# Mixer projections with tokens on partitions and 512 weight columns moving, raw residual in, scaling and turning behind, and a per-boundary table of begin beats

## What is computed

```python
for l in range(2):                                 # first stack
    h = h + 0.5 * swiglu(rmsnorm(h, ffn1_norm[l]), ...)
    z = rmsnorm(h, mix_norm[l]) @ w_in[l]          # 1024 x 5536
    # latent attention (8 heads), differential attention (8 heads), pooling
    branches = einsum('bsnc,ncd->bsnd', [y_mla, y_diff, y_pool], w_branch[l])
    h = h + sum_n(sigmoid(z_gate[n]) * branches[n]) @ w_out[l]
    h = h + 0.5 * swiglu(rmsnorm(h, ffn2_norm[l]), ...)
h = rmsnorm(h, final_norm)
for l in range(2):                                 # second stack
    x = x + 0.5 * rms_norm(swiglu_2(rms_norm(x, pre), ...), post)
    proj = rms_norm(x, ln_mix_pre[l]) @ w_in_2[l]  # windowed attention, mLSTM, RWKV-7
    x = x + rms_norm(concat(y_attn, y_mlstm, y_rwkv) @ w_out_2[l], post)
    x = x + 0.5 * rms_norm(swiglu_2(...), post)
    gate = sigmoid(rms_norm(x, ln_ple_pre[l]) @ w_ple_gate[l])
    x = x + rms_norm(gate * (p[l] @ w_ple_proj[l]), post)
```

## Time and profile before

| | |
|---|---|
| Three runs | 2524.03, 2524.66, 2525.28 us (median 2524.66) |
| The profiled execution | 2525.72 us, its span 2524.4 us |
| PE busy | 2396.8 us, 95% of the span, 13760 matmuls |
| DVE, ACT busy | 1516.1 us (60%), 1224.8 us (49%) |
| Granted TensorE clock, mean | 0.968 |
| Stages, from the ends of the residual's last writes | `mix1` 243.9 and 245.4 us, `mix2` 206.8 and 205.9 us, FFNs 185 to 208 us, `ple` 45.1 and 36.7 us |

### The profile page before, as it was taken

How to read it: one execution, slowest core, us unless ns; L and a number is a source line. 1 busy time by engine, 2 the same in 40 slices (tenths; PEclk the granted TensorE clock), 3 DMA queues, 4 the chain that set the end, 5 groups by cost and what they waited for, 6 DMA issues and landing times.

```text
span 2524.4 us, 33723 instructions
## 1 busy us (share of the span) xinstructions
PE 2396.8 (95%) x13760; PEld 2026.4 (80%) x13760; DVE 1516.1 (60%) x2356; ACT 1224.8 (49%) x2095; POOL 53.7 (2%) x66
## 2 busy tenths in 40 slices
PE   8999999999999999999999979999979997999997
PEld 6788899888888889988788868778857886877885
DVE  4556786555655677755555574755555557476555
ACT  4445454544544555544544443554454444355444
POOL 0000000000000000000000000000000000000000
PEclk9999999999999999999999989799999998979999
DMA  6554345555555433555455532255544552214553
GB/s 238 189 187 155 106 137 189 175 183 197 176 187 182 138 117 132 181 188 197 169 183 185 175 93 91 63 173 181 194 146 160 194 181 87 90 63 171 184 191 113
DMA packets 110746, 400.11 MB, mean 158 GB/s; under 512 B 12288, under 2 KB 12672, under 8 KB 110336
## 3 DMA queue, kind: packets, MB, share of 16 engines
q1 hardware_dynamic: 110592, 397.96, 47.0%
HBM read 396.86 MB, written 1.05 MB: 158 GB/s over the span
## 4 chain that ended last, share of the span: by engine, by line
PE 84%; DVE 10%; ACT 4%; issue 1%; DMA 1%; POOL 0%; SPq 0%; ACTq 0%; DVEq 0%
PE ps L369 75%; DVE wlo L361 3%; PE ps L651 2%; ACT whi L354 1%; PE ps L1814 1%; DVE alo L511 1%; PE ps L1263 1%; ACT ahi L488 1%; PE ps L472 1%; PE ps L1228 1%; PE ps L1247 0%; PE ps L1219 0%; PE ps L2184 0%; DVE xs L767 0%; PE ps L2302 0%
## 5 line engine op out<-in xcount | busy, mean ns | idle before, releaser
L361 DVE TENSOR_TENSOR wlo<-raw,whi 128x1024 fp32r<-128x1024 f32 (+1 forms) x748 | 886.9, 1211 | 172.0 <-ACT whi L354 166.1
L354 ACT CAST whi<-raw 128x1024 fp32r<-128x1024 f32 (+1 forms) x748 | 758.1, 1042 | 125.1 <-PE ps L369 124.7
L369 PE MATMUL ps<-whi,ahi 128*128 128x512 f32 (+2 forms) x1632 | 655.4, 402 | 50.4 <-DVE alo L511 42.5
L369 PE MATMUL ps<-whi,alo 128*128 128x512 f32 (+2 forms) x1632 | 638.4, 391 | 0.0
L369 PE MATMUL ps<-wlo,ahi 128*128 128x512 f32 (+2 forms) x1632 | 637.3, 390 | 0.0
L369 PEld LDWEIGHTS ps<-whi,ahi 128*128 128x128 f32 x1632 | 311.4, 191 | 122.2 <-issue 43.2
L369 PEld LDWEIGHTS ps<-whi,alo 128*128 128x128 f32 x1632 | 310.7, 190 | 63.3
L369 PEld LDWEIGHTS ps<-wlo,ahi 128*128 128x128 f32 x1632 | 312.0, 191 | 56.7
L369 PE MATMUL ps<-whi,yhi 128*128 128x512 f32 (+1 forms) x852 | 335.9, 394 | 0.9 <-DVE wlo L361 0.9
L369 PE MATMUL ps<-whi,ylo 128*128 128x512 f32 (+1 forms) x852 | 332.3, 390 | 0.0
L369 PE MATMUL ps<-wlo,yhi 128*128 128x512 f32 (+1 forms) x852 | 332.2, 390 | 0.0
(11 more groups left out here) (363 smaller groups left out, 2340.2 us busy)
## 6 DMA issues: line engine op xcount, KB each, us to landing
raw<-stream SPq DMA_DIRECT2D x718, 512.0 KB, 4.2
raw<-stream SPq DMA_DIRECT2D x16, 388.0 KB, 2.9
bcb<-bcs SPq DMA_DIRECT2D x9, 512.0 KB, 4.5
raw<-stream SPq DMA_DIRECT2D x8, 416.0 KB, 3.8
raw<-stream SPq DMA_DIRECT2D x4, 384.0 KB, 3.2
cst<-consts SPq DMA_DIRECT2D x1, 1260.0 KB, 8.4
msc<-misc SPq DMA_DIRECT2D x1, 1160.0 KB, 7.5
xs<-xin SPq DMA_DIRECT2D x2, 512.0 KB, 4.3
```

What stands on the lines that cost most here:

```text
L354: act.do.copy(whi[:, n % NSP, 0:w], raw[:, n % NRAW, 0:w]).then_inc(*rounded(n))
L361: dve.do.tensor_tensor(wlo[:, n % NSP, 0:w], raw[:, n % NRAW, 0:w], whi[:, n % NSP, 0:w].bitcast(F), ALU.subtract).then_inc(*rest(n))
L369: m = pe.do.matmul(o, a, b, start=(first and q == 0), stop=(last and q == n - 1))
```

## The change

- `scaled` and `xn` are gone: both mixers turn the raw `xs`, as the FFNs do. The row scale is applied where a projection leaves PSUM (`scale(i)`), in the tanh (`hst`, half the scale) or in the sigmoid.
- All projections of the mixers and `w_branch` have tokens stationary and up to 512 weight columns moving. `pe_column` is gone. The first group of a stage (`pe_first`) does token block 0 over four held pieces, and then block 1.
- What is wanted with features on partitions is turned behind by `pe_chunks`, eight 128 x 128 transposes a call: per layer of `mix1` two calls for query and key, one for pooling, two for `merged`; per layer of `mix2` two for RWKV, one for mLSTM.
- In `mix2` the order of groups is RWKV, mLSTM query and key, attention, mLSTM value and output gate (attention and mLSTM query and key change places); the RWKV columns are reordered in the stream so that a group holds what the front needs first. `cv` takes `bcb`'s place, so `bcb`'s load for `mix2` waits for the mLSTM scores.
- `PLAN` is keyed by boundary and has beats for norm, square, add and post lanes too.

```diff
-    def scaled(s):
-        return PARTS[s][0].startswith("mix")
...
     def pe_norm(s):
...
-                if scaled(s):
-                    src = xn
-                    pe.wait_ge(*((norm_act if hf else norm_dve), s, i))
-                else:
-                    src = xs
-                    wait_x(pe, s, i, hf)
+                wait_x(pe, s, i, hf)
...
-            if scaled(s):
-                yield x_ready(s, i, 1) + 2.1
-                dve.wait_ge(rstd, s, i)
-                dve.do.tensor_scalar(xn[:, i, 0:512], xs[:, i, 0:512], stat[:, 6 + i:7 + i], None,
-                                     ALU.mult).then_inc(*norm_dve(s, i))
...
-    def pe_column(name, l, s, key, col, bank, t, wait):
...
+    def pe_first(name, l, s, key, wd, t):
+
+        held = []
+        for i in range(2):
+            for r in range(4):
+                yield t + wd / 374 * (4 * i + r)
+                if i == 0:
+                    held.append(piece(name, l, (2 * r, 0), wd, 2))
+                    pe.wait_ge(rest, held[r][0])
+                n, w = held[r]
+                pe.wait_ge(a_lo, s, i, max(2 * r + 1, 3))
+                m = gemm(ps[:, i, 0:wd], [(at2(act_pair, ALL, 2 * r + k, slice(128 * i, 128 * i + 128)),
+                                           at2(w, ALL, k, ALL)) for k in range(2)], r == 0, r == 3)
...
+    def pe_chunks(sig, key, src, banks):
+
+        for b in range(2):
+            for c in (2 * b, 2 * b + 1):
+                for i in range(2):
+                    d = 256 * (c % 2) + 128 * i
+                    m = pe.do.transpose(ps[:, banks[b], d:d + 128], src(i)[:, 128 * c:128 * c + 128], ident)
+            m.then_inc(*sig(*key, "turn", b))
...
-        for k, c in enumerate(RWKV):
-            t1 = t + R2 + 2.9 * k
-            yield t1
...
-            pe_column("rwkv_in", l, s, ("rw", c), 128 * c, k % 2, t1, wait)
+        yield from pe_first("rwkv_in", l, s, ("rw", 0), 512, t + R2)
...
+                ("rwkv_in", ("rw", 1), 512, 512, R2 + 10.9, behind(front_act, front_dve, "ru", 0)),
+                ("mqk_in", ("mq",), 0, 512, M2, behind(front_act, front_dve, "ru", 1)),
+                ("attn_in", ("at", 0), 0, 388, A2, behind(lstm_act, lstm_dve, "mt")),
+                ("attn_in", ("at", 1), 388, 388, A2 + 8.6, at_done(0)),
+                ("mvo_in", ("vo",), 0, 512, V2, at_done(1))):
...
+            act.do.mul(ru[:, 2 * g, :], ps[:, 0, :], scale(0)).then_inc(*front_act(s, "ru", g))
...
+            dve.do.tensor_scalar(ru[:, 2 * g + 1, :], ps[:, 1, :], scale(1), None, ALU.mult).then_inc(*front_dve(s, "ru", g))
...
+                act.do.activation(gb[:, i, :], ps[:, i, :], ACT.Tanh, scale=hst[:, i:i + 1]).then_inc(
+                    *gate_act(s, k, i, "tanh"))
...
-            plan = PLAN.get(PARTS[s][0], {}).get(name)
+            plan = PLAN.get(key, {}).get(name, ())
             for k, beat in enumerate(lane):
-                yield org(s) + plan[k] if plan else beat
+                yield org(s) + plan[k] if k < len(plan) else beat
```

More of the change, by code:

```diff
@@ new lines @@
+    "mix2>ffn2_2": {
+        "act_norm": (12.6, 14.26, 23.7, 24.06),
+        "act_post": (3.86, 7.94, 7.94, 16.74),
+        "act_square": (18.56, 18.82, 20.6, 24.92),
+        "dve_norm": (13.64, 14.66, 22.6, 24.16),
+        "dve_post": (10.56, 10.56, 11.68, 12.38, 17.62, 19.64),
+        "dve_square": (21.68, 28.16),
+        "pe_norm": (9.18, 13.62, 22.52, 24.22),
+        "pool_norm": (8.82, 29.24),
+        "pool_post": (1.78, 3.88),
+    },
+    "ple>": {
+        "act_post": (0.54, 4.94, 34.58, 68.04),
+        "dve_post": (-0.54, -0.08, 8.58, 8.62, 29.6, 81.88),
+        "pool_post": (21.02, 24.36),
+    },
@@ L256, in program @@
     stat = place("stat", [16])
+    hst = place("hst", [2])
     rope1 = place("rope1", [2, 64])
@@ L376, in program @@
     HELD = {"ffn1": 3, "ffn2": 3, "mix1": 4, "ffn1_2": 4, "ffn2_2": 4, "mix2": 4, "ple": 4}
-    START = {"mix1": 3.3, "mix2": 9.8, "ple": 1.4}
+    START = {"mix1": 0.3, "mix2": 0.8, "ple": 1.4}
     GU = 2.72
@@ L865, in dve_turn, with scale, pe_wide @@
                                         ALU.subtract).then_inc(*sig(s, name, "ylo", c))
-    def pe_column(name, l, s, key, col, bank, t, wait):
-        n, w = piece(name, l, col, 128, 8)
-        pe.wait_ge(rest, n)
-        wait()
-        gemm(ps[:, bank, 0:256], [(at2(w, ALL, c, ALL), at2(act_pair, ALL, c, ALL))
-                                  for c in range(8)]).then_inc(*dense(s, *key))
-        freed(n, 2.9, dense, s, *key)
-    def pe_wide(name, l, s, key, c, wd, r, banks, t, wait):
-        n, w = piece(name, l, (r, wd * c), wd, 2)
+    def scale(i):
+        return stat[:, 6 + i:7 + i]
+    def pe_wide(name, l, s, key, col, wd, r, banks, t, wait):
+        n, w = piece(name, l, (r, col), wd, 2)
         pe.wait_ge(rest, n)
@@ new lines, in pe_branch1 @@
+                pe_wide("w_in", l, s, ("gate", k), 2464 + 1024 * n + 512 * hh, 512, 2 * r, (0, 1), t1, wait)
+            for b in range(2):
+                yield org(s) + t + 10.9 + 2.72 * b
+                w_n, w = piece("w_branch", (l, n), (2 * b, 512 * hh), 512, 2)
+                pe.wait_ge(rest, w_n)
+                if b == 0:
+                    pe.wait_ge(*Y1[n](s))
+                for i in range(2):
+                    if b == 0 and k:
+                        pe.wait_ge(gate_dve, s, k - 1, i, "gate")
+                    elif b == 0:
+                        pe.wait_ge(pool_dve, s, 2 + i, "y")
+                    m = gemm(ps[:, 2 + i, :], [(at2(y_pair, ALL, 4 * n + 2 * b + q, slice(128 * i, 128 * i + 128)),
+                                                at2(w, ALL, q, ALL)) for q in range(2)], b == 0, b == 1)
+                    m.then_inc(*dense(s, "branch", k, b, i))
+                freed(w_n, 2.72, dense, s, "branch", k, b, 1)
@@ L1513, in y_slot, with act_merged1 @@
+    def act_merged1(s):
+        for k, n, hh, t in branches()[4:]:
+            for b in range(2):
+                yield org(s) + t + 19.4 + 0.7 * b
+                act.wait_ge(gate_pe, s, hh, "turn", b)
+                y = y_slot(4 * hh + 2 * b)
+                act.do.mul(yhi[:, y:y + 2, :], pair(((4, 5), (0, 1))[hh][b]), 0.5).then_inc(*gate_act(s, hh, b, "yhi"))
     def y_slot(d):
@@ new lines, in dve_branch1 @@
+        dve.wait_ge(rstd, s, 1)
+        dve.do.tensor_scalar(hst[:, :], stat[:, 6:8], 0.5, None, ALU.mult).then_inc(*gate_dve(s, "half"))
+        for k, n, hh, t in branches():
+            h = slice(512 * hh, 512 * hh + 512)
+            for i in range(2):
+                yield org(s) + t + 15.4 + 1.3 * i
+                dve.wait_ge(dense, s, "branch", k, 1, i)
+                dve.wait_ge(gate_act, s, k, i, "tanh")
+                first = k < 2
+                if k >= 3:
+                    dve.wait_ge(gate_dve, s, k - 1, i, "sum")
+                dve.do.scalar_tensor_tensor(merged[:, i, h] if first else mb[:, i, :], gb[:, i, :], 1.0, ps[:, 2 + i, :],
+                                            ALU.add, ALU.mult).then_inc(*gate_dve(s, k, i, "gate"))
+                if not first:
+                    dve.wait_ge(gate_dve, s, k, i, "gate")
+                    dve.do.tensor_tensor(merged[:, i, h], merged[:, i, h], mb[:, i, :],
+                                         ALU.add).then_inc(*gate_dve(s, k, i, "sum"))
@@ L1637, in act_project2 @@
+        yield t + M2 + 11.1
+        act.wait_ge(dense, s, "mq", 6, 0)
+        act.do.mul(mt[:, 0, :], ps[:, 0, :], scale(0)).then_inc(*lstm_act(s, "mt"))
+        yield t + 36.2
+        act.wait_ge(lstm_pe, s, "mq", "turn", 0)
+        act.wait_ge(lstm_dve, s, "zero")
+        act.do.copy(mqk[:, 0:2, 3:259], pair(6)).then_inc(*lstm_act(s, "mq"))
         for c in range(2):
```

717 lines of the change are left out of this document (413 added, 304 removed), and 66 rows, old and new, of the table PLAN.

## The result

The changed kernel takes 2439.26 us (median of 4 runs, 2438.37 to 2439.91) against 2524.78 beside it: ratio 0.9661, 95% interval 0.9645 to 0.9678.

A forecast was written before the change was run, and what follows sets the result against it. The prediction took the kernel as bound by PE's matmul stream, with holes at stage entries. Terms A to F summed −4.7 − 12 − 20 − 4 + 7 + 0 = −33.7 us, forecast 2490, range 2466 to 2516.

The forecast's parts named there:

- What bounds the kernel: Whole kernel: bound by PE's stream of matmuls; waits for alo (52.0 us) and xn (13.8) belong to stage entries.
- D: Entries of ple: one wlo instead of two ahead of the last alo, 2 us each, −4; bounds 0 and 5.
- B: Two entries of mix1: raw blocks turned ahead of the last FFN matmuls, no scale awaited; 5.9 us each, −12.
- C: Two entries of mix2: scale and xn leave the chain, twelve block 0 matmuls precede block 1's transposes; 10.0 each, −20.
- A: PE's stream: wide matmuls in 30 groups save 18.7 us, 128 new transposes cost 14.0; net −4.7.
- E: New waits: evictions between wide groups, 0.3 us at 18 places, +5; ru in mix2, 1.1 us each, +2.
- F: Inside of mix2: wait for B_ and the tail taken as unchanged, 0; bounds −10 and +10 a layer.
- cost their length: Rival on the 128 new transposes: each costs 0.3 us instead of 0.11, adding 24, 2514 us; chance 0.03.
- show a wait: Rival, exposed turns: PE waits about 1.1 us at each of 16 transpose calls, adding 15, 2505 us; chance 0.15.
- The pile-up behind the second unit: Rival in mix2: two or three more attention jobs run in series, 22 to 26 us a layer likely, 2537; chance 0.08.
- The tail at full clock: Rival in mix2's attention tail: wide matmuls between jobs keep the clock up, 10 us a layer, 2470; chance 0.15.

The follow-up runs named there:

- e1: Changed kernel with norm, square, add and post lanes by the old formulas at every boundary except mixer entries and around the final norm, ple's lanes too: 2480.0 us, 40.7 slower.
- e12: Changed kernel with the boundary lanes (norm, square, post) by formulas at the exits of both ple stages alone: 2449.3 us, +10.1.
- e14: Changed kernel with norm, square, add and post lanes by formulas at the exits of the four mixers alone: 2456.2 us, +16.9.
- e16: Changed kernel with the boundary lanes by formulas at the program's start and between ffn2 and ffn1 of the first stack: 2442.5 us, +3.2.
- e4: Changed kernel with each of the 128 transposes of the projections' results made twice into the same place: 2446.8 us, +7.6.
- e5: Changed kernel with each 512-column matmul of the mixers' projections and w_branch issued as two of 256 columns: 2453.4 us, +14.1.
- e2: As e1, with formulas at the mixers' entries too (old start beats), so all 16 transposes stand behind the FFN's last matmul: 2499.6 us, 19.6 more than e1.
- e3: As e2, with both mixers' transposes also waiting for their block's row scale, without the scaled copy being made: 2510.1 us, 10.5 more than e2.
- e15: Changed kernel with four unused 512-column matmuls ahead of the transposes of each of mix2's last four attention jobs: 2440.4 us, +1.1.

## Why the prediction was wrong, point by point

**What bounds the kernel: right, and not used.** The earlier trace rows held the answer. 52.0 us of waits for `alo` in 15, "both belong to stage entries", and the prediction then expected 22 of them to go. 17 of the 52 were at the mixers' entries (2 × 3.8 and 2 × 4.7) and 12.1 at `ple`'s (5.3 and 4.8, with 1.0 more behind each). The other 23 were at the start (6.6), around the final norm (2.3), at the exit of `ple` in layer 0 (8.9) and at the exits of `mix2` (5.2), and only 6.2 came back, as waits for `wlo`.

**The step that failed is D, and with it the model of B and C.** D took the table's effect outside the mixers as one `wlo` at `ple`'s entry, −4, with a bound of −10. The diff said that every boundary got beats for norm, square, add and post lanes. e1 puts this at 40.7 us, of which e12, e14 and e16 find 10.1 at `ple`'s exits, 16.9 at the mixers', 3.2 at the start. 9.2 of e14's 16.9 are a cost that only the changed kernel has without its table, so against the kernel before it is about 31. The stage table gives less: 19 us outside the mixers and their entries, 22 with the 3.3 that e12 puts into the FFN behind `ple`, and a part of `mix2`'s 10.2. By either way it is about five times the 4 forecast or more. At `ple`'s entries alone, D's own place, PE's waits for `alo` fell by 4.5 and 3.9 us (2 each forecast). The prediction named the exit of `mix2`, as a model, and no other exit, and put a price on none.

The second part of the miss is in the first step of the way above: some 24 us for the `xn` copies, the form, the order of groups and the lanes inside the mixers. The sum has A + E + F = +2 for these, and the `xn` copies only as an unnamed part of B and C. Which of them gave it stays open.

**A, the stream: right.** The counts are as forecast, and each form's usual spacing is the same in both traces (0.120, 0.227 and 0.109 us), so the stream is 4.8 us shorter, against −4.7. In e4 and e5 a half to two thirds of such time reached the end, which the sum did not allow for.

**B, `mix1`'s entries: somewhat small.** −12 forecast. The FFNs ahead give 3.6 and 4.2, and of what half clock cost inside `mix1`, about 4 us a layer by the traces, all is gone in layer 0 and more than half in layer 1. PE is busy for 20.00 of 20 us at clock 1.00. e2 puts the order at these entries at 12.7 us.

**C, `mix2`'s entries: right in its mechanism, its size too small.** −20 forecast; the FFNs ahead are 15.7 and 16.3 shorter, 3.3 of the latter at `ple`'s exit by e12. The term left 3.3 us of stalls open for block 1 behind twelve matmuls; in fact there are 24 of block 0, twelve ahead of the turn and twelve behind, and 0.56 us is left. The exit of `mix2` with its 2.59 was taken as what the form can reach; it was itself a boundary ordered by formula. e2 and e3 show what made the entries long: at `mix2`'s the order 9.5 us and the wait for the scale 9.1 in the FFNs ahead.

**E, new waits: half right.** Not one wait for an eviction between gate groups appears (5 charged). The waits for `ru` are 2 × 2.1 for the bank and 2 × 0.9 for the turn, 6.1 in all against 2.2. What the term did not have is the rise of the waits for `wlo`, 6.3 to 12.8 us.

**F, the inside of `mix2`: wrong by a part.** Forecast 0, measured −4.9 and −5.3 a layer with the exit. PE's wait ahead of the first transposes of `B_` in the changed kernel, against 3.73 in the earlier trace rows:

```profile
1460.25 0.30 PE L2035 MATMUL ps<-cst,B__119 128*128 128x128 f32 x1 [0.99 <-DVE rw L1854]
```

It went from 3.73 us, for `B_`, to 0.99, for `rw`. The place itself lies later, 40.8 us behind the stage's first matmul (1460.25 − 1419.44) where it was 32.6 (1497.19 − 1464.55): the front comes later, as F said, and PE has more projections to do before it. How the 4.9 and 5.3 split between the inside and the exit was not taken apart.

**The rivals.** The turns do not cost their length (e4), and only the two of `mix2`'s first calls show a wait, 0.94 us each. The pile-up behind the second unit didn't come: the order moved as foreseen, all eight jobs stand behind it, but their spacing shrank. The scores of the last three jobs in the changed kernel, against 9.1 us in the earlier trace rows:

```profile
1543.23 0.79 PE L2361 MATMUL ps<-qkT 64*128 64x256 f32 x4 [1.39 <-DVE S L2417]
1552.95 0.79 PE L2361 MATMUL ps<-qkT 64*128 64x256 f32 x1
...
1558.12 1.23 PE L2361 MATMUL ps<-qkT 64*128 64x256 f32 x4
```

One gap of 9.7 us remains and the last is 5.2. The last score stands 1558.12 − 1419.44 = 138.7 us behind the stage's first matmul, where it stood 138.6 before (1603.17 − 1464.55): two jobs more behind the second unit, in the same time. So the 9.1 us that I had read as the chain of a job cannot be that; that it was the distance at which the other work had been placed fits, and is not shown. The tail at full clock did not come either.

**Chances.** Faster was right at 0.87, and for the reasons that B and C gave. The range of 2466 to 2516 was built from the terms' own bounds and the rivals' sums, and a term that isn't there has no bound.

## What to carry to other kernels

When a change replaces the rule that orders work at every boundary, list all boundaries of the program with their idle time before and cost each one, also those that the change's first words don't name; here the table of waits had them in one row. A boundary that serves as a model for another must not be touched by the same change. A part taken off the new kernel measures what it is worth there, which is not always what it gained over the old one: look at the same place in the old trace before adding it up. And where a stage's second block comes late from the norm, don't start with both blocks in turn: hold the first pieces, finish block 0 over all of them, and let block 1's norm run under it (10 us a layer in `mix2`).

## What the runs showed of the hardware

A 128-column transpose has a length of 0.272 us and a spacing of 0.109, however many stand in a row (16 in e4). Splitting a 512-column matmul into two of 256, each with its own weight load, costs 0.013 us of stream (2 × 0.120 − 0.227). In a stretch at half clock, sixteen matmuls whose results are not used cost 0.7 to 2.2 us in all, while the granted clock of that window rose from 0.51 to 0.69 (e15); in the changed kernel PE was busy for 36 of those 38 us and still had half the clock.
